# RWKV doubling levels 4, 8 and 16 as 32x32x32 products on four row groups, with the transposed inverse summed in PSUM

## What is computed

```
def frame(state, inp):
    r_t, w_t, k_t, v_t, kk_t, kka_t = inp
    sa = jnp.einsum('bhvk,bhk->bhv', state, kk_t)
    state = (state * w_t[:, :, None, :] - sa[..., None] * kka_t[:, :, None, :]
             + v_t[..., None] * k_t[:, :, None, :])
    return state, jnp.einsum('bhvk,bhk->bhv', state, r_t)
```

## Time and profile before

| | us |
|---|---|
| median of three runs | 2974.82 |
| profiled execution | 2979.43 |
| its span (first to last instruction) | 2977.6 |
| PE busy (share of the span) | 2888.0 (97%) |
| DVE busy | 1663.8 (56%) |
| ACT busy | 1279.9 (43%) |
| POOL busy | 132.7 (4%) |
| L2276 and L2229 (dense layers) in the chain that ended last | 29% and 26% |
| L2672 (`each`) in the same chain | 2% |

### The profile page before, as it was taken

The page is one execution under the profiler, slowest core; times in us unless marked ns, Lnnn a source line. Parts: engine busy times, 40 slices in busy tenths (PEclk is TensorE's granted clock), DMA queues, the critical chain, the costliest instruction groups (busy, mean ns, idle before and its releaser), DMA issues.

```text
span 2977.6 us, 50952 instructions
## 1 busy us (share of the span) xinstructions
PE 2888.0 (97%) x22340; PEld 2662.0 (89%) x22340; DVE 1663.8 (56%) x1484; ACT 1279.9 (43%) x1210; POOL 132.7 (4%) x111
## 2 busy tenths in 40 slices
PE   6899999999999999999999999999999999999998
PEld 5899987899889997889999889999888998899887
DVE  7878987795444454455455654444745444444444
ACT  3334444444434543346354544444344443344433
POOL 0011110000000000000022320000000000000000
PEclk8789999999999999999999999999999999999999
DMA  9999768596556665545451016556554555566553
GB/s 353 384 313 307 265 224 309 178 364 226 189 192 194 190 195 183 195 168 184 152 173 68 10 45 198 191 190 225 170 189 140 194 195 188 196 190 193 184 188 123
DMA packets 300453, 596.74 MB, mean 200 GB/s; under 512 B 12144, under 2 KB 17776, under 8 KB 299760
## 3 DMA queue, kind: packets, MB, share of 16 engines
q1 hardware_dynamic: 294864, 587.83, 58.6%
q10 hardware_dynamic: 5408, 6.23, 0.8%
HBM read 583.80 MB, written 6.29 MB: 198 GB/s over the span
## 4 chain that ended last, share of the span: by engine, by line
PE 84%; DVE 7%; ACT 3%; DMA 3%; issue 2%; POOL 0%; SPq 0%; ACTq 0%; DVEq 0%
PE ps L2276 29%; PE ps L2229 26%; PE ps L2792 9%; PE ps L2376 4%; PE ps L2391 2%; DVE ada_acc L1483 2%; DVE wL L1325 2%; PE ps L2913 2%; ACT wH L765 2%; PE ps L2672 2%; PE ps L2352 1%; DMA ada<-w_ada 1%; DMA raw<-w_up 1%; PE ps L2253 1%; PE ps L2471 1%
## 5 line engine op out<-in xcount | busy, mean ns | idle before, releaser
L1325 DVE TENSOR_TENSOR wL<-raw,wH 128x2048 fp32r<-128x2048 f32 x436 | 1004.2, 2303 | 1120.2 <-ACT wH L765 1115.9
L765 ACT ACTIVATE wH<-raw 128x2048 fp32r<-128x2048 f32 x436 | 837.7, 1921 | 1262.9 <-PE ps L2229 456.5
L2276 PE MATMUL ps<-actH,wH 128*128 128x256 f32 x2816 | 779.6, 277 | 4.0 <-DVE wL L1325 3.9
L2276 PE MATMUL ps<-actL,wH 128*128 128x256 f32 x2816 | 777.9, 276 | 0.0
L2276 PE MATMUL ps<-actH,wL 128*128 128x256 f32 x2816 | 777.8, 276 | 0.0
L2276 PEld LDWEIGHTS ps<-actH,wH 128*128 128x128 f32 x2816 | 529.2, 188 | 6.3 <-DVE wL L1325 3.3
L2276 PEld LDWEIGHTS ps<-actL,wH 128*128 128x128 f32 x2816 | 529.3, 188 | 0.1
L2276 PEld LDWEIGHTS ps<-actH,wL 128*128 128x128 f32 x2816 | 529.1, 188 | 0.0
L2229 PE MATMUL ps<-wH,hidH 128*128 128x512 f32 x1024 | 403.4, 394 | 1.3 <-DVE wL L1325 1.3
L2229 PE MATMUL ps<-wH,hidL 128*128 128x512 f32 x1024 | 400.4, 391 | 0.0
L2229 PE MATMUL ps<-wL,hidH 128*128 128x512 f32 x1024 | 397.4, 388 | 0.0
(11 more groups left out here) (419 smaller groups left out, 3670.0 us busy)
## 6 DMA issues: line engine op xcount, KB each, us to landing
raw<-w_in SPq DMA_DIRECT2D x96, 1024.0 KB, 5.1
ada<-w_ada SPq DMA_DIRECT2D x80, 1024.0 KB, 8.3
raw<-w_up SPq DMA_DIRECT2D x64, 1024.0 KB, 5.3
raw<-w_down SPq DMA_DIRECT2D x64, 1024.0 KB, 5.1
raw<-w_mlp_up SPq DMA_DIRECT2D x64, 1024.0 KB, 5.3
raw<-w_mlp_down SPq DMA_DIRECT2D x64, 1024.0 KB, 5.1
raw<-w_gates SPq DMA_DIRECT2D x48, 1024.0 KB, 5.2
raw<-w_o SPq DMA_DIRECT2D x16, 1024.0 KB, 6.9
```

The costliest lines, as they stand in the source:

```text
L765: nc.scalar.activation(wH[:, s % SPLIT if L[name]["spg"] > 1 else r % SPLIT, :, :], raw[:, slot, :, :], ACT.Copy).then_inc(wh_ready, 1)
L1325: nc.vector.tensor_tensor(wL[:, b, :, :], raw[:, slot, :, :], wH[:, b, :, :].bitcast(F32), ALU.subtract).then_inc(wl_ready, 1)
L2276: ins = nc.tensor.matmul(out, w[:, b, k, cols], v[:, kk, :], start=(kk == 0 and j == 0 and n % 2 == 0), stop=(kk == STEP_K * spg - 1 and j ...
```

## The change

- `each` takes a size. For v = 2, 3 and 4 it is 32: a level up to 32 is block-diagonal in blocks of 32, so only the four diagonal 32x32 blocks of each pair of chunks are multiplied. A call makes 16 products of 32x32x32, each on its own 32 partitions (four row groups, with the column group of the same number), and leaves the other blocks of the bank alone. For v = 1 and 5 it stays 64, with 8 products.
- The first Y goes to a tile of its own, `Y1`, which is kept through the turn. The dY products clear their bank only at v = 1 and add to it afterwards, and DVE forms `Ym` = `Y1` + the sum in PSUM.

```diff
--- before.py
+++ after.py
@@ -328,7 +328,7 @@
     rtok = ring("rtok", [P, TT, RJ, P])
     rtop[0] += LOW_AT
     uf, ST = ring("uf", [P, RHEADS * RHEAD]), ring("ST", [P, RJ, P])
-    Bc = ring("Bc", [P, MATS, 2, CHUNK])
+    Bc, Y1 = ring("Bc", [P, MATS, 2, CHUNK]), ring("Y1", [P, MATS, CHUNK])
     LW, BT, KTt = (lw0, lw, lw, lw), (BT0, BT1, BT1, BT1), (KT0, KT1, KT1, KT1)
     rr, rk, rvv, d0, d1, d2, sg, aa, gg, cs, Gd, Gi = (
         at(n, [P, RJ, T], F32, R0 + 2 * K1 * j) for j, n in enumerate(
@@ -1878,13 +1878,13 @@
                     masks(0, Bc, range(2 * f, 2 * f + 2))
                     dve.wait_ge(mat_masked, 8 * i + 2 * f + 2)
                     link(nc.vector.tensor_tensor(Ym[:, m4, :], Bc[:, m4, 0, :], level(0, RHEADS), ALU.mult))
-                    nc.vector.tensor_tensor(Ym[:, m4, :], Ym[:, m4, :], chunk_ident.unsqueeze(1).to_broadcast([P, RHEADS, CHUNK]),
+                    nc.vector.tensor_tensor(Y1[:, m4, :], Ym[:, m4, :], chunk_ident.unsqueeze(1).to_broadcast([P, RHEADS, CHUNK]),
                                             ALU.add).then_inc(y1_ready, 1)
                 masks(1, Kc, range(RHEADS))
                 for v in range(1, len(LEVELS)):
                     for f, m4 in enumerate(HALVES):
                         dve.wait_ge(dy_done, 10 * i + 2 * v - 1 + f)
-                        nc.vector.tensor_tensor(flat(Ym[:, m4, :]), flat(Ym[:, m4, :]), ps[:, 4 + f, 0:RHEADS * CHUNK], ALU.add
+                        nc.vector.tensor_tensor(flat(Ym[:, m4, :]), flat(Y1[:, m4, :]), ps[:, 4 + f, 0:RHEADS * CHUNK], ALU.add
                                                 ).then_inc(y_level, 1)
                     if v == 1 and more:
                         shifted(i + 1, 0)
@@ -2664,12 +2664,13 @@
                                                        skip_group_check=True)
                         ins.then_inc(mat_done, 1)
 
-                def each(f, out, lhs, rhs_, fresh=True):
+                def each(f, out, lhs, rhs_, fresh=True, size=CHUNK):
 
                     for m in range(4 * f, 4 * f + 4):
-                        for c in range(2):
-                            rows, cols = chunk_rows(c), slice(m % 4 * CHUNK, (m % 4 + 1) * CHUNK)
-                            ins = nc.tensor.matmul(ps[rows, out + f, cols], lhs[rows, m, :], rhs_[rows, m, :],
+                        for c in range(P // size):
+                            rows, part = slice(c * size, (c + 1) * size), slice(c * size % CHUNK, c * size % CHUNK + size)
+                            cols = slice(m % 4 * CHUNK + part.start, m % 4 * CHUNK + part.stop)
+                            ins = nc.tensor.matmul(ps[rows, out + f, cols], lhs[rows, m, part], rhs_[rows, m, part],
                                                    start=(fresh and m % 4 == 0), stop=True, skip_group_check=True)
                     return ins
 
@@ -2691,10 +2692,11 @@
                     for m in range(4 * f, 4 * f + 4):
                         for c in range(2):
                             rows, cols = chunk_rows(c), slice(m % 4 * CHUNK, (m % 4 + 1) * CHUNK)
-                            ins = nc.tensor.matmul(ps[rows, 2 + f, cols], Ym[rows, m, :], ident[rows, rows],
+                            ins = nc.tensor.matmul(ps[rows, 2 + f, cols], Y1[rows, m, :], ident[rows, rows],
                                                    start=(m % 4 == 0), stop=False, skip_group_check=True)
                     ins.then_inc(x1_done, 1)
                 for v in range(1, len(LEVELS)):
+                    size, Y = 2 * LEVELS[4] if 1 < v < 5 else CHUNK, Y1 if v == 1 else Ym
                     for f in range(2):
 
                         pe.wait_ge(lm_ready, 6 * i + v + (f if v == 1 else 1))
@@ -2702,7 +2704,7 @@
                             pe.wait_ge(x_level, 8 * i + 2 * v - 3 + f)
                         else:
                             pe.wait_ge(x1_ready, 2 * i + f + 1)
-                        each(f, 0, Lm[:, v % 2, :, :], Xm).then_inc(w1_done, 1)
+                        each(f, 0, Lm[:, v % 2, :, :], Xm, size=size).then_inc(w1_done, 1)
                     if v == 1:
 
                         pe.wait_ge(mat_masked, 8 * i + 8)
@@ -2723,8 +2725,8 @@
                         if v > 1:
                             pe.wait_ge(y_level, 10 * i + 2 * v - 3 + f)
                         if v < len(LEVELS) - 1:
-                            each(f, 2, Ym, W1, fresh=False).then_inc(dx_done, 1)
-                        each(f, 4, W1, Ym).then_inc(dy_done, 1)
+                            each(f, 2, Y, W1, fresh=False, size=size).then_inc(dx_done, 1)
+                        each(f, 4, W1, Y, fresh=(v == 1), size=size).then_inc(dy_done, 1)
                     if v == 1 and i:
                         variance(i - 1)
 
```

## The result

The changed kernel takes 3014.64 us (median of 4 runs, 3014.01 to 3017.17); beside it the kernel before took 2976.99 (4 runs, 2969.61 to 2979.34). The ratio is 1.0127, with a 95% interval of 1.0111 to 1.0144. So it is slower by 38 us where 9 us less was forecast, and outside the range. The profiled execution took 3014.01 us, 34.6 more than that of before.

A forecast was written before the change was run, and what follows sets the result against it. TensorE, 84% of the chain, was taken as the bound. Gains of 0.8 us in turn 0, 2.7 each in turns 1 and 2 and 3.0 in turn 3 sum to 9.2: median 2974.82 to 2965.6 us, range 2961 to 2982.

The forecast's parts named there:

- The size of a call: TensorE calls in levels 2, 3 and 4: 0.27 us instead of 0.47, four row groups side by side.
- Rival (a): Matmul starts bound the calls: a loss above 14.7 ns per pair; at 19.5 ns +11 us, 2986; chance 0.14.
- rival (b): Calls: pairs take 9 to 14 ns, or only two or three groups overlap; gain 0 to 8 us; chance 0.22.
- A level at full clock: One doubling level in the turns takes 2.04 us instead of 3.03 where nothing else is late.
- the sum of 9.2 us: Total gain over the four RWKV turns: 0.8 + 2 x 2.7 + 3.0 us.
- the 2.7 us behind the squares: Turns 1 and 2: key sums start 2.7 us earlier each, limited at level 4 by ACT's key squares.
- the 3.0 of turn 3: Turn 3, without rk, kk or squares: last Ym sum of level 4 comes 0.2 + 1.0 + 1.0 + 0.8 us earlier.
- PSUM, Y1, DVE: Writing and adding to Y1, and dY products not clearing their bank except at level 1, cost nothing by themselves.
- What reaches the end: Turn-by-turn step: shorter calls gain only until DVE, ACT or POOL is late next; 9.2 us remain.
- Rival (c): Gaps in the levels lower TensorE's clock; one fall per turn costs 6 us, giving 2972; chance 0.06.
- A granted clock under 1.00 between 1612 and 1780: Sign in the profile after, over the turns, that the forecast was wrong in the clock.
- The forecast case: Shorter calls in the turns gain 9.2 us; median 2965.6 us, spanning 2961 to 2969; chance 0.55.

The follow-up runs named there:

- e2: Changed kernel with every second 32x32 product of levels 4, 8 and 16 left out, so part is not computed; 2987.75 us, ratio 1.0043.
- e3: Changed kernel with three of four 32x32 products of levels 4, 8 and 16 left out, so part is not computed; 2984.6 us, ratio 1.0029.
- e1: Changed kernel with every product back at size 64, leaving only Y1 and the dY sums in PSUM; 2978.41 us, ratio 1.0009.
- e6: Changed kernel with 64-row products at levels 4, 8 and 16, each made as two of 32 weight columns; all computed; 2998.06 us, ratio 1.0079.
- e8: Kernel with sums in PSUM and 64x64x64 products, chunk 1 left out at levels 4, 8 and 16; 2993.41 us, ratio 1.0057.
- e5: e2 plus one unread 128x128x256 product per level, between the W calls and the next wait; 2979.88 us, ratio 1.002.
- e7: Changed kernel with 64x64x64 products at levels 4, 8 and 16, and only the nonzero 32x32 quadrant at level 32; 2979.08 us, ratio 1.0003.
- e4: Changed kernel with 32x32x32 products at level 16 only, the others at 64; all computed; 2996.99 us, ratio 1.0057.

## Why the prediction was wrong

**The size of a call: right.** 0.27 us forecast at 32x32, 0.27 measured (1678.51 to 1678.78), with 32 matmuls in it: 8.4 ns from one start to the next. Rival (a), with its 14.7 ns as the point where it turns, and rival (b), 9 to 14 ns or too few groups side by side, are both out as limits inside a call. The Trainium skill's floor of about 25 ns, which the prediction read as the pace of one tile, is indeed no floor across row groups: after starts matmuls three times as densely.

**A level at full clock, and the sum of 9.2 us: right as far as they go.** 2.04 us forecast, 1.96 measured in e2. In after 0.97 to dX and four calls of 0.27 would be 2.05. At equal clock e2 and e3 are 10 and 9 us faster than before, so, as far as that estimate goes, 9.2 is what shorter calls give where nothing halts and the clock holds. How it was made up turn by turn (the 2.7 us behind the squares, the 3.0 of turn 3) no trace shows, since the clock fell in every turn of both.

**PSUM, Y1, DVE: right.** e1 is before.

**What reaches the end: wrong.** This is the step that failed. The sum asked of each shorter call what was late next, and looked for it among DVE, ACT and POOL. It left out that PE's own instructions have to arrive, a term put at nothing, and the halts for them measured 23.1 us. The risk could have been seen: the diff doubles the instructions of three levels, from 192 to 384 each, while before's levels already took 192 in 3.03 us, 63 per us, and the instruction queue stands on the page. Its price could not, since before has no such halt. The prediction used "every pair doubles" only for the rate at which pairs start (rival a), a limit inside the engine, and read the answer from a stretch of three pairs in 58 ns. Such a short burst can't show a limit that sets in after hundreds of instructions: 65 per us is 31 ns a pair, above the 19.5 ns of rival (a). At 65 per us, 3 x 384 instructions take 17.7 us; the levels of after took A = 15.60, and I read the difference as what had been fetched ahead.

**The clock: mechanism named, size and chance wrong.** Rival (c) had the clock at 0.06 and at 6 us; it cost some 24. Its argument was that a turn with gaps had kept 1.00. But gaps were not what mattered, as e6 shows from one side and e8 from the other. "A granted clock under 1.00 between 1612 and 1780" was the sign named for this, and it came. The forecast case had the clock at 1.00 throughout, a second term at nothing.

**The account of the 38 us.** The runs of after have 176 us at half clock in the mean, those of before 110. The 66 us between them cost 24 us at 0.36 each, and 14 are left at equal clock. Halts of 23.1 less the forecast gain of 9.2 are 14 too. The traces give the same picture less exactly. The turns are 35.6 us longer (201.7 against 166.1, over the stretch in which half clock is counted); 23.1 - 9.2 + 68.9 x 0.36 is 38.7, 3 us too much. The terms aren't independent: some of the time at half clock PE stood waiting for instructions anyway. The price of 0.36 has two checks in the turns themselves: e1, with before's products, takes 6.1 us longer for 17.9 at half clock (0.34), and e8, whose calls at full clock are as long as before's, 26.0 for 62.3 (0.42).

**Still open.** What the clock's gate measures is not settled; the runs only show in which levels it fell. A kernel with the small products spread out so that instructions keep up, and the clock held up, wasn't made: e2 shows that the clock still falls with half the instructions, and e5 that this filler holds it only in some runs. And the levels of before stand at 63 instructions per us with no halt; whether they would run into the limit if they were a little faster was not tried.

## What to carry to other kernels

Before splitting products into smaller tiles, divide the instructions of the stretch (two for each fp32 pair) by its hoped-for time: above 65 per us over more than a few hundred instructions, PE halted here for 0.5 to 2.3 us every 254, and the halts (23.1 us) took more than the shorter products gave (9 us). Look at "issue" in the waits, in the middle of a call, as the sign of it. Then ask what the clock does when each instruction uses less of the array: a gain of 1 us per level is gone after 3 us at half clock (0.36 each), and the levels in the profile of the unchanged kernel gave no sign of it. And where runs of one kernel differ in their mean clock, compare kernels at equal clock: e2's gain of 10 us and e7's of 2 can be seen only so.

## What the runs showed of the hardware

- PE's instructions come in packets of 16 KB, 3.5 to 4 us apart in the levels of after; some 65 to 71 per us is what PE got when it ran dry (after, e4, e6). A burst of 98 per us over one level ran without a halt (e2).
- Four row groups take matmuls 8.4 ns apart (after), and fp32 pairs of 32x32 tiles run at some 0.033 us per pair and row group whether one, two or four groups work (a call of 8 pairs per group in 0.26 to 0.27 us in e3, e2 and after).
- The clock fell to half 1.1 us after the first products on one 64x64 tile (e8), where PE had been busy 11.56 of the last 12.1 us; in before it stayed at full at the same place with 11.55, and in e6 in a stretch where PE was busy 14.05 of 18 us with 64x32 tiles.
- An execution takes 0.36 us longer for each us at half clock (65 runs of the kernel before).
- The fall comes with the changed levels in most turns (22 of 24), and its length can be very much the same: 13.6 to 13.7 us in each of turns 0 to 2 in the traces of e2 and e3.
